# The order of TensorE's products from expert 4 on: down-projections taken one expert later in a mixture-of-experts layer

## The chip, the cores and the metric

The kernel runs on one core of one Trainium2 chip. The metric is the device time of one execution in microseconds (us).

## The reference, cut to what matters

One decoder layer on 256 tokens of width 1024, in float32: a recurrent branch and an attention branch, merged, and then a mixture of 32 experts of which each token takes four. For this case only the experts matter. Per expert, on the tokens routed to it:

```
gu = xb @ w_gu[e] + b_gu[e]                      # w_gu[e]: 1024 x 2048
x_glu = jnp.minimum(gu[:, :D_EXPERT], SWIGLU_LIMIT)
x_lin = jnp.clip(gu[:, D_EXPERT:], -SWIGLU_LIMIT, SWIGLU_LIMIT)
act = x_glu * jax.nn.sigmoid(SWIGLU_ALPHA * x_glu) * (x_lin + 1.0)
return act @ w_down[e] + b_down[e]               # w_down[e]: 1024 x 1024
```

The results are weighted by the router's gates and added up per token.

## The kernel before

The branches come first (products in split float32, weights passing through a landing buffer). From about 280 us on the kernel is a loop over the 32 experts, numbered 0 to 31. Every expert has 64 slots for its tokens; a further pass exists for more and isn't taken here.

**Buffers.** An expert's gate-and-up weights (`gu`, 8 MB) lie in one of two sets, by the parity of the expert, each of two halves of 4 MB. The down weights (`dn`, 4 MB) have one set only, of two halves of 2 MB, which every expert uses.

**The queue of weights.** SP issues all loads, in one order written out by hand (L348 to L352): `gu` of expert 2i, `dn` of 2i-1, `gu` of 2i+1, `dn` of 2i. Ahead of each half it waits until that half's buffer has been read: for `gu` (`load_gu`, L277) on `gu_used`, which TensorE counts up at each quarter of `up`, and for `dn` (`load_dn`, L285) on `dn_used`, counted up at each half of `down`. A wait holds all that stands behind it in SP's program. Experts 0 to 3 have `gu` loads of their own (`load_early`, L269), issued by quarters.

**TensorE** takes per expert e these groups; the lines are those in the profile:

- `up`: the bias (L668), then 32 products with `gu` (L680, 64 records), into banks 4 and 5
- `turn_weights` (L689): two transposes of the weighted selection, which ScalarE copies to `wT`
- `gather` (L620): 48 small products that fetch the tokens of expert e+1, which VectorE copies to `xg`
- `turn_act` (L695): four transposes of the activation, which VectorE made from banks 4 and 5 and then copies to `actT`
- `down`: two halves of 8 products with `dn` (L701, 32 records in all), into bank 6, which ScalarE copies to `y_sb`
- `combine` (L654): the result of the expert before, weighted, into banks 0 to 3

**Two orders.** Up to expert 21 TensorE runs `expert` (L706): `up(e)`, turns and gather, the combine of e-1, and then `down(e)`, for which it waits on weights that lie in the queue behind `gu` of e+1. From expert 22 on it runs `step` (L738): `up(e)`, the gather, then `down(e-1)`, then the turns and the combine of e-1; so `down(e)` stands behind `up(e+1)`, as in the queue. The first step has no `down`. `last_step` ends the loop with expert 31, whose down weights have buffers of their own. ScalarE has the same two bodies (L1003 and L1024), and VectorE the same work in both, with the gather's result in bank 6 or 7. The constant `STEPS` says at which expert the second order begins, on all three engines. SP doesn't use it.

Of the kernel before, what the change touches and what calls it, by code (L numbers as in the profile page):

```python
# [43 lines left out]
ALPHA = 1.702  # L44
CONV = 4
LAND = 2
STEPS = 22
LAST_ROWS = ((0, 2), (2, 3), (3, 4))
N_BLK = 20
PIECES = 4  # L50
# [8 lines left out]
def program(nc, x, vecs, rope, w_in, lru_wx, lru_wa, w_proj_rnn, w_proj_attn, w_out,  # L59
# [7 lines left out]
    with ctx:  # L67
# [176 lines left out]
        def most_rows(eng):  # L244

            eng.wait_ge(count_ready, 1)
            return eng.value_load(cnt_i[0:1, 0:1], min_val=0, max_val=T)
# [175 lines left out]
        def _(pe):  # L423
            mm = nc.tensor.matmul

            def keep_clock(bank, n):

                for _ in range(n):
                    mm(ps[:, bank, :], ones[:, :], ones[:, :].unsqueeze(1).to_broadcast([P, 4, P]),
                       start=True, stop=True)  # L430
# [185 lines left out]
            def gather(buf, bank=6):  # L616

                for k in range(KT):
                    for n, (t, q) in enumerate((t, q) for t in range(TT) for q in range(3)):
                        last = mm(ps[:, bank, k * SLOTS:(k + 1) * SLOTS], part[q][:, t, k * P:(k + 1) * P],  # L620
                                  sel[buf][:, t, :], start=n == 0, stop=n == 3 * TT - 1)
                last.then_inc(gathered, 1)
# [28 lines left out]
            def combine(par, t, y=y_sb, stop=False):  # L651

                for h in range(2):
                    last = mm(ps[:, 2 * t + h, :], wT[par][64 * h:64 * h + 64, t * P:(t + 1) * P],  # L654
                              y[64 * h:64 * h + 64, :], start=False, stop=stop)
                return last

            def up(E, X, par, first=False, early=0):

                if first:  # L660
                    pe.wait_ge(xg_half, 1)
                else:
                    pe.wait_ge(xg_ready, X + (par + 1))
                pe.wait_ge(gu_read, E + (par + 1))
                for c in range(2):
                    for h in range(2):
                        rows = slice(32 * (2 * c + h), 32 * (2 * c + h) + 32)
                        mm(ps[64 * h:64 * h + 64, 4 + c, :], bsel[par][rows, :], b4[rows, :], start=True, stop=False)  # L668
                for m in range(4):
                    if early:  # L670
                        pe.wait_ge(early_landed[par][m], 16 * early)
                    elif m % 2 == 0:
                        pe.wait_ge(gu_landed[par][m // 2], 8 * E - 16)
                    if first and m == 2:
                        pe.wait_ge(xg_ready, 1)
                    for r in range(2):
                        k = 2 * m + r
                        for c in range(2):
                            for h in range(2):
                                last = mm(ps[64 * h:64 * h + 64, 4 + c, :], xg[:, k * SLOTS:(k + 1) * SLOTS],  # L680
                                          gu[par][m // 2][:, m % 2 * 2 + r, c * D + h * HALF:c * D + (h + 1) * HALF],
                                          start=False, stop=k == KT - 1)
                    last.then_inc(gu_used, 1)

            def turn_weights(X, par, bank=7):
                pe.wait_ge(parts_ready, TT)
                pe.wait_ge(sel_ready, X + (par + 1))
                for t in range(TT):
                    last = nc.tensor.transpose(ps[:, bank, t * P:(t + 1) * P], sel_g[par][:, t, :], ident[:, :])  # L689
                last.then_inc(wT_filled, 1)  # L690

            def turn_act(E, par):
                pe.wait_ge(act_ready, E + (par + 1))
                for j in range(4):
                    last = nc.tensor.transpose(ps[:, 7, j * P:(j + 1) * P], act_s[:, j * P:(j + 1) * P], ident[:, :])  # L695
                last.then_inc(actT_filled, 1)

            def down(half, bank=6, src=actT, js=range(DN_RUN), dn=dn):
                for j in js:
                    for h in range(2):  # L700
                        last = mm(ps[64 * h:64 * h + 64, bank, :], src[:, j, half * SLOTS:(half + 1) * SLOTS],  # L701
                                  dn[half][:, j, h * HALF:(h + 1) * HALF],
                                  start=half == 0 and j == 0, stop=half == 1 and j == DN_RUN - 1)
                return last

            def expert(E, X, par, meanwhile=None, first=False, at_once=False, early=0):  # L706

                up(E, X, par, first, early)  # L710
                turn_weights(X, par)
                pe.wait_ge(sel_ready, X + (par + 2))
                if not first:
                    pe.wait_ge(y_ready, E + par)
                gather(1 - par)
                pe.wait_ge(wT_ready, E + (par + 1))
                if meanwhile:
                    meanwhile()
                elif at_once:
                    keep_clock(7, 5)  # L720
                if not (first or at_once):
                    combine(1 - par, 0)
                turn_act(E, par)
                if first or at_once:
                    keep_clock(4, 3)
                else:
                    combine(1 - par, 1)
                pe.wait_ge(actT_ready, E + (par + 1))
                pe.wait_ge(xg_ready, X + (par + 2))
                for half in range(2):  # L730
                    pe.wait_ge(dn_landed[half], 16 * E + 16 * (par + 1) - 16 * at_once)
                    down(half).then_inc(dn_used, 1)
                if at_once:
                    pe.wait_ge(y_ready, E + (par + 1))
                    combine(par, 0)
                    combine(par, 1)

            def step(E, par, first=False):  # L738

                pe.wait_ge(wT_ready, E + par)  # L740
                up(E, E, par)
                pe.wait_ge(actT_ready, E + par)
                pe.wait_ge(sel_ready, E + (par + 2))
                gather(1 - par, 7)
                if not first:
                    for half in range(2):
                        pe.wait_ge(dn_landed[half], 16 * (E + par))
                        down(half).then_inc(dn_used, 1)
                pe.wait_ge(gu_read, E + (par + 2))
                turn_weights(E, par, 5)  # L750
                pe.wait_ge(xg_ready, E + (par + 2))
                turn_act(E, par)
                pe.wait_ge(y_ready, E + par)
                combine(1 - par, 0)
                combine(1 - par, 1)
# [30 lines left out]
            most = most_rows(pe)  # L786
            for par in range(2):
                expert(2, 2, par, early=2)
            with pe.Fori(2, STEPS // 2, 1) as i:
                for par in range(2):  # L790
                    expert(2 * i, 2 * i, par)
            step(STEPS, 0, first=True)
            step(STEPS, 1)
            with pe.Fori(STEPS // 2 + 1, N_E // 2 - 1, 1) as i:
                for par in range(2):
# [23 lines left out]
        def _(act):  # L819
# [199 lines left out]
            most = most_rows(act)  # L1019
            with act.Fori(1, STEPS // 2, 1) as i:  # L1020
                for par in range(2):
                    expert(2 * i, par)

            def step(E, par, first=False):  # L1024
                act.wait_ge(glu_ready, E + (par + 1))
                A(act_s[:, :], g1[:, :], ACT.Sigmoid, scale=ALPHA).then_inc(sig_ready, 1)  # L1026
                if not first:
                    act.wait_ge(dn_used, 2 * E + 2 * par)
                    A(y_sb[:, :], ps[:, 6, :], ACT.Copy).then_inc(y_ready, 1)
                act.wait_ge(wT_filled, E + (par + 1))  # L1030
                A(wT[par][:, :], ps[:, 5, 0:T], ACT.Copy).then_inc(wT_ready, 1)

            step(STEPS, 0, first=True)
            step(STEPS, 1)
# [454 lines left out]
```

## Time and profile before

| | us |
|---|---|
| median of 3 runs | 1199.77 (1198.56 to 1199.92) |
| the profiled execution | 1201.84 |
| its span, first to last instruction | 1200.1 |
| TensorE busy in the span | 1131.4 (94%) |
| VectorE busy | 348.4 (29%) |
| ScalarE busy | 218.6 (18%) |
| mean rate of all DMA | 375 GB/s |

Times in the rows are microseconds from the first instruction. PE is TensorE's products, PEld its weight loads, DVE is VectorE, ACT is ScalarE, SPq is SP's queue. A busy span of TensorE is modelled at its end. The chain of waits is followed back from the last instruction, at each step to what released it. Durations come from this one execution, whose own time is 2.07 us above the median.

### The profile page before, as it was taken

To read this page: it belongs to the slowest core of one execution; us is meant where nothing else is said; L and a number is where in the kernel's file an instruction comes from. 1 tells how busy PE (TensorE), PEld (TensorE's weight loads), DVE (VectorE), ACT (ScalarE), POOL (GpSimd) and SP (SyncE) were. 2 spreads that over 40 slices of the span, in tenths; PEclk is the share of its full clock that TensorE was granted. 3 is DMA by queue.
4 is the path that set the end of the run, shared out by engine and by line. 5 is a ranking of instruction groups with operands and counts; after the bars stand their busy time and mean duration, and the time that the engine had idled before them with its cause. 6 is when DMAs were issued, how large, how long until landed. Compare 5 with 4: busy or idle time off the path is not lost.

```text
span 1200.1 us, 17281 instructions
## 1 busy us (share of the span) xinstructions
PE 1131.4 (94%) x7486; PEld 579.1 (48%) x7486; DVE 348.4 (29%) x667; ACT 218.6 (18%) x359; POOL 5.4 (0%) x20
## 2 busy tenths in 40 slices
PE   8999999999999999999999999999999999999997
PEld 8999899995333333333333333333333333333332
DVE  6747775655221111111111111111111211111112
ACT  5557456444000000000000000000000000000002
POOL 1000000000000000000000000000000000000000
PEclk9999999999999999999999999999999999999999
DMA  9635455798999999999999999999999999999994
GB/s 272 218 142 162 164 219 200 266 361 350 419 413 428 434 429 428 435 428 430 431 429 433 430 427 435 428 428 431 431 430 429 421 428 432 431 429 430 433 428 196
DMA packets 47708, 449.70 MB, mean 375 GB/s; under 512 B 6321, under 2 KB 9457, under 8 KB 30193
## 3 DMA queue, kind: packets, MB, share of 16 engines
q1 hardware_dynamic: 47104, 447.70, 89.5%
q10 hardware_dynamic: 416, 0.83, 0.4%
q8 instruction: 35, 0.57, 0.2%
q0 software_dynamic: 144, 0.52, 0.1%
q14 instruction: 9, 0.07, 0.0%
HBM read 447.48 MB, written 1.05 MB: 374 GB/s over the span
## 4 chain that ended last, share of the span: by engine, by line
PE 49%; DMA 44%; DVE 4%; ACT 2%; issue 1%; SPq 0%; ACTq 0%; DVEq 0%; POOL 0%; POOLq 0%
DMA dn<-in_w_down 34%; PE ps L680 14%; PE ps L701 13%; DMA gu<-in_w_gu 10%; PE ps L456 4%; PE ps L452 4%; PE ps L453 4%; PE ps L654 1%; PE ps L620 1%; DVE w_lo L1106 1%; PE ps L668 1%; PE ps L471 1%; PE ps L472 1%; PE ps L476 1%; PE ps L435 1%
## 5 line engine op out<-in xcount | busy, mean ns | idle before, releaser
L680 PE MATMUL ps<-gu,xg 128*64 128x512 f32 x2048 | 450.9, 597 | 10.2 <-DMA gu<-in_w_gu 10.0
L680 PEld LDWEIGHTS ps<-gu,xg 128*64 128x64 f32 x2048 | 144.5, 138 | 314.5 <-issue 297.3
L701 PE MATMUL ps<-dn,actT 128*64 128x512 f32 x992 | 223.5, 597 | 39.5 <-DMA dn<-in_w_down 39.3
L1398 DVE TENSOR_SCALAR g<-ps 128x512 f32<-128x512 f32 x32 | 22.1, 692 | 674.5 <-PE ps L680 674.5
L701 PEld LDWEIGHTS ps<-dn,actT 128*64 128x64 f32 x992 | 66.9, 137 | 186.7 <-issue 115.9
L1106 DVE TENSOR_TENSOR w_lo<-land,w_hi 128x1024 fp32r<-128x1024 f32 x80 | 94.6, 1219 | 64.1 <-ACT w_hi L842 64.1
L452 PE MATMUL ps<-x_hi,w_hi 128*128 128x256 f32 x384 | 96.3, 288 | 2.4 <-ACTq L880 2.4
L453 PE MATMUL ps<-x_lo,w_hi 128*128 128x256 f32 x384 | 94.8, 284 | 0.0
L842 ACT ACTIVATE w_hi<-land 128x1024 fp32r<-128x1024 f32 x80 | 80.1, 1052 | 51.7 <-PE ps L456 32.7
L452 PEld LDWEIGHTS ps<-x_hi,w_hi 128*128 128x128 f32 x384 | 74.1, 193 | 2.8 <-ACTq L880 2.6
L453 PEld LDWEIGHTS ps<-x_lo,w_hi 128*128 128x128 f32 x384 | 74.1, 193 | 0.1
L654 PE MATMUL ps<-y_sb,wT 64*128 64x512 f32 x248 | 67.6, 633 | 0.7 <-ACT y_sb L1046 0.7
L1005 ACT ACTIVATE wT<-ps 128x256 f32<-128x256 f32 x22 | 8.4, 384 | 317.9 <-PE ps L689 317.9
L1011 ACT ACTIVATE y_sb<-ps 128x512 f32<-128x512 f32 x22 | 13.1, 597 | 271.7 <-PE ps L701 271.7
L456 PE MATMUL ps<-x_hi,w_lo 128*128 128x256 f32 x384 | 54.7, 286 | 0.0
L620 PEld LDWEIGHTS ps<-sel,part 128*128 128x128 bf16 x1488 | 46.9, 98 | 7.6 <-issue 7.3
L456 PEld LDWEIGHTS ps<-x_hi,w_lo 128*128 128x128 f32 x384 | 50.3, 195 | 0.0
L620 PE MATMUL ps<-sel,part 128*128 128x64 bf16 x1488 | 48.5, 193 | 0.0
L1409 DVE COPY actT<-ps 128x512 f32<-128x512 f32 x31 | 21.4, 691 | 55.9 <-PE ps L695 53.5
L1026 ACT ACTIVATE act_s<-g 128x512 f32<-128x512 f32 x9 | 5.7, 630 | 166.9 <-DVE g L1398 166.9
L668 PE MATMUL ps<-b,bsel 32*64 32x512 f32 x256 | 34.8, 613 | 0.0
L654 PEld LDWEIGHTS ps<-y_sb,wT 64*128 64x128 f32 x248 | 19.4, 185 | 13.5 <-issue 9.5
(258 smaller groups left out, 836.8 us busy)
## 6 DMA issues: line engine op xcount, KB each, us to landing
gu<-in_w_gu SPq DMA_DIRECT2D x56, 4096.0 KB, 28.5
dn<-in_w_down SPq DMA_DIRECT2D x62, 2048.0 KB, 25.3
gu<-in_w_gu SPq DMA_DIRECT2D x16, 2048.0 KB, 13.5
land<-in_w_in SPq DMA_DIRECT2D x13, 2048.0 KB, 8.4
land<-in_w_proj_rnn SPq DMA_DIRECT2D x2, 2048.0 KB, 9.1
land<-in_w_proj_attn SPq DMA_DIRECT2D x2, 2048.0 KB, 9.9
land<-in_w_out SPq DMA_DIRECT2D x2, 2048.0 KB, 7.8
dn_last<-in_w_down SPq DMA_DIRECT2D x1, 2048.0 KB, 26.7
```

The costliest lines, as they stand in the source:

```text
L452: mm(to, w_hi[:, b, k, :], src_hi[:, k, :], start=k == 0, stop=False)
L453: mm(to, w_hi[:, b, k, :], src_lo[:, k, :], start=False, stop=False)
L456: last = mm(to, w_lo[:, b, k, :], src_hi[:, k, :], start=False, stop=k == KT - 1)
L620: last = mm(ps[:, bank, k * SLOTS:(k + 1) * SLOTS], part[q][:, t, k * P:(k + 1) * P], sel[buf][:, t, :], start=n == 0, stop=n == 3 * TT - 1)
L654: last = mm(ps[:, 2 * t + h, :], wT[par][64 * h:64 * h + 64, t * P:(t + 1) * P], y[64 * h:64 * h + 64, :], start=False, stop=stop)
L668: mm(ps[64 * h:64 * h + 64, 4 + c, :], bsel[par][rows, :], b4[rows, :], start=True, stop=False)
L680: last = mm(ps[64 * h:64 * h + 64, 4 + c, :], xg[:, k * SLOTS:(k + 1) * SLOTS], gu[par][m // 2][:, m % 2 * 2 + r, c * D + h * HALF:c * D + ...
L701: last = mm(ps[64 * h:64 * h + 64, bank, :], src[:, j, half * SLOTS:(half + 1) * SLOTS], dn[half][:, j, h * HALF:(h + 1) * HALF], start=ha ...
L842: A(w_hi[:, q % PIECES], land[u % LAND][:, :, (q % PIECES) * P:(q % PIECES + 1) * P], ACT.Copy).then_inc(hi_ready, 1)
L1106: V.tensor_tensor(w_lo[:, p], land[q // PIECES % LAND][:, :, p * P:(p + 1) * P], w_hi[:, p].bitcast(f32), ALU.subtract).then_inc(lo_ready, 1)
L1398: V.tensor_scalar(by_rows(g1[:, :]), by_columns(ps[:, 4, :]), LIMIT, None, ALU.min).then_inc(glu_ready, 1)
L1409: V.tensor_copy(to[:, :, :], ps[:, 7, :].rearrange("p (j s) -> p j s", j=4)).then_inc(actT_ready, 1)
```

## The change

The constant goes from 22 to 4, and TensorE's loop over the pairs of experts 4 to 21 in the first order goes, as it would be empty. Experts 2 and 3 stay in the first order. On ScalarE and VectorE the loop bounds follow from the constant: their first loop then holds experts 2 and 3 alone, and the second one the pairs from 4 or 6 on.

```diff
@@ -44,7 +44,7 @@
 CONV = 4
 LAND = 2
-STEPS = 22
+STEPS = 4
 LAST_ROWS = ((0, 2), (2, 3), (3, 4))
@@ -786,9 +786,6 @@
             for par in range(2):
                 expert(2, 2, par, early=2)
-            with pe.Fori(2, STEPS // 2, 1) as i:
-                for par in range(2):
-                    expert(2 * i, 2 * i, par)
             step(STEPS, 0, first=True)
             step(STEPS, 1)
             with pe.Fori(STEPS // 2 + 1, N_E // 2 - 1, 1) as i:
```

## Rows read from the trace of the kernel before

**Rows 1.** The page: what the DMA engines moved, in 40 equal slices of 30 us.
```profile
GB/s 272 218 142 162 164 219 200 266 361 350 419 413 428 434 429 428 435 428 430 431 429 433 430 427 435 428 428 431 431 430 429 421 428 432 431 429 430 433 428 196
```

**Rows 2.** The chain that ended last: start, length, what (L701 `down`, L680 `up`).
```profile
500.90 3.68 PE ps L701 x16
...
884.74 25.34 DMA dn<-in_w_down
910.12 3.65 PE ps L701 x16
...
1047.96 7.09 PE ps L680 x32
...
1125.03 39.78 DMA gu<-in_w_gu
1164.85 8.63 PE ps L680 x32
```

**Rows 3.** Timeline of TensorE, experts 4 and 5: start, length, instructions.
```profile
394.03 13.95 PE L680 MATMUL ps<-gu,xg 128*64 128x512 f32 x64
...
412.47 7.09 PE L701 MATMUL ps<-dn,actT 128*64 128x512 f32 x32
...
420.51 13.95 PE L680 MATMUL ps<-gu,xg 128*64 128x512 f32 x64
```

**Rows 4.** Timeline of TensorE, experts 22 to 24, in the second order.
```profile
914.72 13.95 PE L680 MATMUL ps<-gu,xg 128*64 128x512 f32 x64
...
935.64 13.95 PE L680 MATMUL ps<-gu,xg 128*64 128x512 f32 x64
...
951.03 7.09 PE L701 MATMUL ps<-dn,actT 128*64 128x512 f32 x32
...
961.79 13.96 PE L680 MATMUL ps<-gu,xg 128*64 128x512 f32 x64
```

**Rows 5.** Timeline of SP's queue, `dn` of experts 23 and 24.
```profile
954.90 3.75 SPq L285 DMA_DIRECT2D dn<-in_w_down  x2
...
981.01 3.77 SPq L285 DMA_DIRECT2D dn<-in_w_down  x2
```

**Rows 6.** Timeline of SP's queue, `dn` of expert 5.
```profile
416.34 3.75 SPq L285 DMA_DIRECT2D dn<-in_w_down  x2
```

**Rows 7.** Tile `gu`, 408 to 409 us: expert 6's second half, issue to landing.
```profile
L277 SPq DMA_DIRECT2D gu<-in_w_gu x1: 333/333/333, 408.2 to 408.2; - x1
...
DMA to landing us min/median/max: 24.5/24.5/24.5
```

**Rows 8.** Tile `dn`, 247.5 to 248.5 us: a half of expert 0.
```profile
L285 SPq DMA_DIRECT2D dn<-in_w_down x1: 347/347/347, 247.9 to 247.9; - x1
...
DMA to landing us min/median/max: 7.6/7.6/7.6
```

**Rows 9.** Tile `dn`, 416 to 417 us: expert 5's first half.
```profile
L285 SPq DMA_DIRECT2D dn<-in_w_down x1: 333/333/333, 416.3 to 416.3; - x1
...
DMA to landing us min/median/max: 21.2/21.2/21.2
```

**Rows 10.** Tile `dn`, 340 to 341 us, and below it `gu`, 348 to 349.
```profile
L285 SPq DMA_DIRECT2D dn<-in_w_down x1: 328/328/328, 340.2 to 340.2; - x1
...
DMA to landing us min/median/max: 12.0/12.0/12.0
...
L277 SPq DMA_DIRECT2D gu<-in_w_gu x1: 353/353/353, 348.4 to 348.4; - x1
...
DMA to landing us min/median/max: 16.1/16.1/16.1
```

**Rows 11.** Timeline of TensorE, second halves of `up` of experts 28 and 29.
```profile
1077.18 7.09 PE L680 MATMUL ps<-gu,xg 128*64 128x512 f32 x32 [2.63 <-DMA gu<-in_w_gu]
...
1106.42 8.78 PE L680 MATMUL ps<-gu,xg 128*64 128x512 f32 x32 [2.63 <-DMA gu<-in_w_gu]
```

**Rows 12.** Window 1106.4 to 1108: busy times, PEclk granted, DMA share, GB/s.
```profile
1106.40:1108.00 1.60, 1.58 (x4) 0.44 (x6) 0.00 (x0) 0.00 (x0) 0.00 (x0) 0.55 1.11 471
```

## The prediction

> **What bounds the kernel now.** I read three views in turn. The page's slices say what is full: from the eleventh slice on, 300 us, each slice but the last moves 413 to 435 GB/s [rows 1], the flat ceiling of the expert loop. So the first question for any change here is whether it lets this stream pause. The chain of waits says who ends last in each stretch. Over experts 7 to 21 it repeats one pair: a `dn` transfer, then the second half of `down` that waited for it [rows 2]. Those waits end at 500.90 for expert 7 and at 910.12 for expert 21: 409.22 us for 14 experts, 29.23 us each. That is the pace of the weights: three equal parts of 4 MB a turn, so 9.74 us for 4 MB and 4.87 us for 2 MB. Near the end the chain goes through `gu` transfers to 1164.85, where TensorE starts the second half of expert 31's gate-and-up product; what follows is a fixed tail [rows 2].
>
> The timeline of TensorE says what an expert costs it when nothing is late. In the old order `up` of expert 4 starts at 394.03 and that of expert 5 at 420.51: 26.48 us [rows 3]. In the new order, experts 23 to 24, it is 961.79 - 935.64 = 26.15 us [rows 4]. Both are under 29.23, so from expert 7 on TensorE waits for weights in either order, and its order can't shorten the stream. It can only lengthen it, by freeing a buffer too late, or change the tail.
>
> **The change part by part.** Experts 4 to 21 leave the old body for the new one. The products per expert are the same (64 records of `up`, 32 of `down`, 48 of the gather and so on), no DMA is added or dropped, and the last experts already run in the new order. The moved step is `down(e)`: from before `up(e+1)` to behind it. What it releases, `dn_used`, is what SP waits for ahead of the next `dn` issue, and behind that wait in SP's program stand the next two `gu` halves. So a late `down` holds back 12 MB of transfers, even where the `gu` buffers have long been free.
>
> *The steady part* costs nothing. In the new order before, SP issues the `dn` halves of successive turns at 954.90 and 981.01, 26.11 us apart, faster than the weights' 29.23 [rows 5], so SP gains about 3.1 us of lead per turn until TensorE is held by weights again. The 0.33 us a turn that TensorE saves lies under that wait.
>
> *The first turns* are the matter, because at expert 4 TensorE is still behind the weights. Where is the new release? `up(4)` keeps its start of 394.03. The short first step takes 935.64 - 914.72 = 20.92 us [rows 4], so `up(5)` starts at 414.95 in place of 420.51. `down(4)` comes 951.03 - 935.64 = 15.39 us later, at 430.34 in place of 412.47 [rows 3, 4]. SP issues `dn(5)` 954.90 - 951.03 = 3.87 us after `down` starts [rows 4, 5], at 434.21 in place of 416.34 [rows 6]. When is the queue empty? The last transfer ahead, the second half of `gu(6)`, is issued at 408.2 and lands 24.5 us later, at 432.7 [rows 7]; it is released by `up(4)`, which doesn't move. So the queue runs dry 1.5 us before the next issue. Then `dn(5)` restarts it cold. A 2 MB `dn` half issued at 247.9, just as the queue had emptied, took 7.6 us to land [rows 8], against 4.87 behind other transfers; so it lands at 441.8. In the old order it landed at 416.3 + 21.2 = 437.5 [rows 9]. **First term: +4.3 us.**
>
> The Trainium skill (DMA: Bandwidth & Descriptors, section "Anatomy of one DMA") gives a transfer a fixed part of about 2.0 us beside its bytes, most of it the receipt after the last byte. By that page 2 MB would land after 6.8 us (an estimate), the term would be 3.5 us, and since a receipt doesn't delay the transfer behind it, the stream itself would lose less still. The row's 7.6 us is this kernel's own and I keep it.
>
> *The thin queue after a restart.* A queue that is short, though not empty, also lost time. At the switch by expert 22 the weights' own schedule puts the end of `gu(24)` at 910.12 plus four halves of `gu` (experts 23 and 24) and two of `dn(22)`, that is 910.12 + 4 x 9.74 + 2 x 4.87 = 958.8; `dn(23)` was issued at 954.90, a lead of 3.9 us. The stream lost something even so: from 910.12 to the landing of `gu(27)`'s second half, which TensorE waited for until 1047.96, lie ten `gu` halves and eight `dn` halves, 97.4 + 39.0 = 136.4 us, and it took 137.84. **That is 1.4 us lost at today's switch** [rows 2, 5], and the second issue's lead of 7 to 8 us (981.01 against 988.0) is within it. A worse case is expert 4's `gu`: issued at 348.4, when the `dn` ahead of it landed at 340.2 + 12.0 = 352.2, it landed at 364.5 [rows 10]: 12.3 us for a transfer of 9.74, so 2.6 us lost with 3.8 us of lead.
>
> After the restart, `dn(5)`'s second half and the two halves of `gu(7)` are issued within some 5 us with leads of 4 us and up, as at 954.90. Between 0 (the thin part is already in the cold restart) and 2.6 I take 1.4, the case with the same code. **Second term: +1.4 us.** The next turn: `up(6)` starts at 414.95 + 26.15 = 441.10, so `dn(6)` is issued at 441.10 + 15.39 + 3.87 = 460.4. The queue, shifted by 5.7 us, holds work to 461.9 + 5.7 = 467.6 (461.9 is 442.4 for `dn(5)`'s second half plus two `gu` halves). The lead is 7.2 us, like the second issue at today's switch, whose cost is in the 1.4; at most another 1.4. The turn after that has 10 us, and it grows.
>
> **Third term: -1.4 us**, today's loss at expert 22, which goes away, since there TensorE already waits for weights in the new order and SP's issues are far ahead of the stream.
>
> Sum: 4.3 + 1.4 - 1.4 = **+4.3 us**. Nothing later takes it back: from 442 to 1164 the stream is full, and the tail hangs on its last pieces. Against the profiled execution's own 1201.84 us (span 1200.1) that gives 1206.1; that execution is 2.1 us above the median of the runs shown. On the median, 1199.77 + 4.3 = **1204.1**.
>
> *The tail and the clock.* With one long wait per turn in place of two short ones, TensorE stood idle 2.63 us in mid-`up`. After one such gap, at 1077.18, the half took 7.09 us; after another, at 1106.42, it took 8.78 [rows 11]; in the slow stretch the granted clock was 0.55, close to the lower of its two levels, 1.2 against 2.4 GHz [rows 12]. Expert 31's half took 8.63 [rows 2]. In mid-loop the 1.7 us hide under the 3.1 us of slack; in the last half they are on the path. I expect it in the new kernel as well, and so no difference; but if it falls away there it gives back 1.5 us. [...]
>
> **The rivals.** *The queue doesn't miss it.* TensorE's late release is covered, or the switch costs the same 1.4 us wherever it stands: then 1199.8, or 1198.3 without the last dip. For it: today's switch costs 1.4. Against it: there the lead was 3.9 us, here it is -1.5, and 1.5 comes from rows in direct sequence; this case holds from the point where `dn(5)` is issued before 432.7 - 3.9 = 428.8. *Faster*: the new order at 22 had cost its 1.4 and this goes, the pause at expert 5 is absorbed, and the last half runs at the full clock: 1.4 + 1.5 = 2.9, so 1196.9. It needs a queue that is fed past 434 by what is now behind the wait; rows 7 speak against it. *A deeper pause*: each of the next two issues loses like the worst row, 4.3 + 2.6 + 1.4 - 1.4 = 6.9, so 1206.7; for it: three issues in a row with leads under 8 us; against it: only the first was seen to lose much. *The clock falls at every expert*, and in both halves of `up`: 1.6 us each, 26.15 + 3.2 = 29.35 a turn, just over the weights' 29.23, so about 0.1 us a turn for 25 turns, +3 us on top: 1207. [...]
>
> **How the numbers follow.** Forecast 62%; not missed 24%; faster 5%; deeper pause 7%; clock 2%. The forecast's own bounds are 4.3 + 0 - 1.4 = 2.9, less 1.5 for the tail, so 1.4 (1201.2), and 6.9 (1206.7). To leave no more than 2 in 10 out, the range goes down past the second case's 1199.8, to 1199.0, and up to 1207.0, which takes the deeper pause in. No change can be told from 0.2%, that is 2.4 us, so slower begins at 1202.2. The forecast with the tail's 1.5 off is 1202.6, still above; its low corner isn't. Slower 0.68, same 0.27, faster 0.05.
>
> **What would show it.** In the changed kernel: `up(5)` at 415, `down(4)` at 430.3, SP's `dn` issue at 434.2 where 416.34 stood; a hole of about 2 us or more in the DMA share after 432; the landing of that half at 441.8 or later; from about expert 8 on, a second half of `up` that waits for `gu`, every 29.2 us, and the last of these, expert 31's, about 4 us behind 1164.85. If no hole is there, or the wait for `gu(31)` ends within 1 us of 1164.85, the forecast is wrong; if the hole is there and the end isn't later, then something in the stream was not at its ceiling.

## The result and the profile after

The changed kernel took 1205.15 us, the median of 6 runs (1201.81 to 1207.55), beside 1199.76 for the kernel before on the same chip: ratio 1.0048, interval 1.0032 to 1.0064. On another chip, in the run e8 below, it was 1.0037 (1.0021 to 1.0052). So the change makes the kernel slower, by 5.4 us on the first chip and 4.1 on the second, by the medians; the forecast was +4.3.

The profiled execution of the changed kernel was its fastest, 1201.81 us with a span of 1200.0, no longer than the span before. Its trace must therefore be read by differences. First the page's 30 us slices:

```profile
GB/s 271 221 141 179 186 215 203 242 389 349 423 410 433 430 338 434 432 426 434 434 426 434 433 427 433 431 428 434 427 430 428 432 430 430 430 430 431 431 429 226
```

One slice stands out against [rows 1]: the fifteenth, 420 to 450 us, with 338 GB/s where 429 stood. The timeline of TensorE there:

```profile
391.00 13.95 PE L680 MATMUL ps<-gu,xg 128*64 128x512 f32 x64
...
411.92 13.95 PE L680 MATMUL ps<-gu,xg 128*64 128x512 f32 x64
...
427.31 3.23 PE L701 MATMUL ps<-dn,actT 128*64 128x512 f32 x14
```

In this execution `up(4)`, the first of these rows, starts 3.03 us earlier than in [rows 3]. From there on the steps are those of [rows 4] to 0.01 us: 20.92 to `up(5)`, 15.39 to `down(4)`. SP's queue:

```profile
398.28 7.19 SPq L277 DMA_DIRECT2D gu<-in_w_gu  x2
431.18 3.75 SPq L285 DMA_DIRECT2D dn<-in_w_down  x2
435.18 0.85 SPq L277 DMA_DIRECT2D gu<-in_w_gu  x2
```

No `dn` issue stands between the `gu` of expert 6 and 431.18; before there was one at 416.34 [rows 6]. The tiles by single windows, the last `gu` ahead and the first `dn` behind:

```profile
L277 SPq DMA_DIRECT2D gu<-in_w_gu x1: 333/333/333, 405.1 to 405.1; - x1
...
DMA to landing us min/median/max: 24.6/24.6/24.6
```

```profile
L285 SPq DMA_DIRECT2D dn<-in_w_down x1: 333/333/333, 431.2 to 431.2; - x1
...
DMA to landing us min/median/max: 7.8/7.8/7.8
```

The queue's last transfer lands at 405.1 + 24.6 = 429.7, and the next is issued 1.5 us later, at 431.2. It lands at 439.0 (438.9 by the unrounded times). The windows of 1 us show the hole itself; the last three columns are the granted clock, the DMA share and GB/s. A packet is counted in the window in which it starts:

```profile
427.00:428.00 1.00, 1.00 (x17) 0.60 (x15) 0.93 (x3) 0.28 (x1) 0.00 (x0) 1.00 0.15 49
428.00:429.00 1.00, 1.00 (x6) 0.29 (x4) 1.00 (x2) 0.00 (x0) 0.00 (x0) 1.00 0.00 0
429.00:430.00 1.00, 1.00 (x8) 0.35 (x6) 0.26 (x1) 0.00 (x0) 0.00 (x0) 1.00 0.00 0
430.00:431.00 1.00, 1.00 (x8) 0.37 (x6) 0.00 (x0) 0.00 (x0) 0.00 (x0) 1.00 0.00 0
431.00:432.00 1.00, 1.00 (x6) 0.29 (x4) 0.00 (x0) 0.00 (x0) 0.00 (x0) 1.00 0.00 0
432.00:433.00 1.00, 1.00 (x8) 0.35 (x6) 0.00 (x0) 0.00 (x0) 0.00 (x0) 1.00 1.22 229
```

In four windows no packet starts, while TensorE is busy in all of them. By the packets' own times in the trace nothing is in flight from 429.2 to 432.15, 2.9 us. By TensorE's own row nothing is wrong here.

What the stream lost: with 3.03 us taken off, the old order's landing of `dn(5)` would be 437.5 - 3.0 = 434.5, so it is 4.4 us late. `gu(7)` then landed at 454.4, 15.5 us after that `dn` half, where 4.87 + 9.74 = 14.6 are its due, and `dn(6)`'s second half came another 0.5 late. In all the stream is 5.8 us behind by 480, and then keeps its pace to the end:

```profile
1126.01 39.97 DMA gu<-in_w_gu
1166.02 7.09 PE ps L680 x32
```

The last wait for `gu` ends at 1166.02, 1.17 us after 1164.85 [rows 2]: 5.8 lost at expert 5, 1.4 not lost at expert 22, 3.0 gained ahead of the loop, which makes +1.4; 0.2 is what my readings leave. The profile of e8, which starts its loop when the kernel before does, has this wait end at 1168.70, 3.85 us behind 1164.85, where the prediction put it "about 4 us" behind:

```profile
1168.70 8.78 PE ps L680 x32
```
The 3.0 us ahead of the loop in the first profile aren't the change's: no code there differs. They go with the clock. These windows are of the changed kernel, and then of the kernel before:

```profile
10.00:20.00 10.00, 7.96 (x66) 7.72 (x65) 9.55 (x23) 8.54 (x16) 0.00 (x0) 1.00 1.12 334
...
120.00:140.00 20.00, 17.04 (x139) 16.73 (x138) 17.68 (x22) 8.71 (x12) 0.00 (x0) 1.00 0.50 180
```

```profile
10.00:20.00 10.00, 7.59 (x51) 7.35 (x50) 9.59 (x25) 7.21 (x13) 0.00 (x0) 0.83 1.13 333
120.00:140.00 20.00, 17.05 (x126) 16.48 (x126) 17.67 (x22) 9.92 (x12) 0.00 (x0) 0.91 0.58 205
```

A granted clock of 0.83 over 10 us and of 0.91 over 20 us is about 1.7 us of full clock withheld each time, 3.4 in all before, and nothing after. The twelve traces of this case agree: in the first 280 us six have nothing withheld, and `up(0)` starts at 281.1 to 281.7; three have 1.7 us, and it starts at 282.4 to 283.2; two have 3.4, 284.1 and 284.3; one has 5.1, 285.4. And expert 31's half took 7.09 us after against 8.63 before: another 1.5. So this one execution had luck worth about 4.5 us, which hides the change in its span. The median of the runs doesn't have it.

### The profile page after: what moved, and what is told of

Same layout as the page of the kernel before. It is cut to its first block, busy times and chain, and to the rows that moved or that the text cites. A ratio compares the mean times of both kernels' runs of the same rounds, so it can differ in the third digit from the quotient of the medians.

```text
span 1200.0 us, 17253 instructions
## 1 busy us (share of the span) xinstructions
PE 1132.4 (94%) x7486; PEld 578.5 (48%) x7486; DVE 348.5 (29%) x667; ACT 217.0 (18%) x359; POOL 5.4 (0%) x20
## 4 chain that ended last, share of the span: by engine, by line
PE 54%; DMA 38%; DVE 4%; ACT 2%; SPq 1%; issue 1%; ACTq 0%; DVEq 0%
DMA gu<-in_w_gu 37%; PE ps L680 19%; PE ps L701 12%; PE ps L452 4%; PE ps L456 4%; PE ps L453 4%; PE ps L620 2%; PE ps L654 1%; DVE w_lo L1103 1%; PE ps L668 1%; PE ps L476 1%; PE ps L471 1%; PE ps L472 1%; ACT w_hi L839 1%; SPq L277 0%
## 5 line engine op out<-in xcount | busy, mean ns | idle before, releaser
L680 PE MATMUL ps<-gu,xg 128*64 128x512 f32 x2048 | 465.9, 610 | 47.2 <-DMA gu<-in_w_gu 46.7
L680 PEld LDWEIGHTS ps<-gu,xg 128*64 128x64 f32 x2048 | 145.6, 140 | 366.1 <-issue 287.8
L701 PE MATMUL ps<-dn,actT 128*64 128x512 f32 x992 | 219.9, 595 | 0.1
L701 PEld LDWEIGHTS ps<-dn,actT 128*64 128x64 f32 x992 | 68.5, 137 | 128.3 <-issue 124.1
L1023 ACT ACTIVATE act_s<-g 128x512 f32<-128x512 f32 x27 | 17.0, 630 | 535.7 <-DVE g L1395 535.7
L654 PE MATMUL ps<-y_sb,wT 64*128 64x512 f32 x248 | 62.7, 618 | 0.7 <-ACT y_sb L1043 0.7
L1026 ACT ACTIVATE y_sb<-ps 128x512 f32<-128x512 f32 x26 | 15.5, 598 | 186.3 <-PE ps L701 186.3
L1398 DVE SCALAR_TENSOR_TENSOR l<-l,g 128x512 f32<-128x512 f32 x32 | 22.1, 692 | 1.1
```

The lines of the kernel that those rows point to most:

```text
L1398: V.scalar_tensor_tensor(out=l1[:, :], in0=l1[:, :], scalar=1.0, in1=g1[:, :], op0=ALU.add, op1=ALU.mult).then_inc(t_ready, 1)
```

## The experiments

Each ratio is to the kernel before on the same chip. The first four ran together, then the next four, then the last two.

**Switch two experts later (e1_steps6).**

```diff
-STEPS = 22
+STEPS = 6
```

> STEPS = 6 in the kernel before: the new order two experts later. Dry-queue theory: the lead of the first late dn issue grows by 29.23 - 26.48 = 2.75 us per expert, so from -1.5 us (switch at 4) to about +4, the same as at 22 (3.9): no hole, and the time of the kernel before within 0.2%, 1199 to 1201.5 us. Rival, the new order itself costs in each of its experts (clock falls, waits inside up): 26 of the 28 experts of the changed kernel still run in it, so about +5 us, 1204 to 1205.

Measured: 1200.09 us, ratio 1.0008 (0.9996 to 1.0020). Moving the switch by two experts takes most or all of the loss away, though 26 of 28 experts run in the new order. The expected lead of 4 us wasn't there in the profile: `dn` was issued at 486.0, with the queue's last landing at 487.4, a lead of 1.4, and that half came 2.3 us late.

```profile
L285 SPq DMA_DIRECT2D dn<-in_w_down x1: 333/333/333, 486.0 to 486.0; - x1
...
DMA to landing us min/median/max: 8.6/8.6/8.6
```

Some 1.6 us of the missing 2.6 are in the first step. It took 466.72 - 444.16 = 22.56 us in place of 20.92, and a window in it shows the clock lowered:

```profile
460.00:470.00 10.00, 8.44 (x36) 2.91 (x38) 3.09 (x9) 0.36 (x1) 0.00 (x0) 0.83 1.03 439
```

Another 0.8 is that the stream had lost less before expert 4: 1.9 us late there in this trace, 2.6 in the kernel before. With 2.3 late at the switch and 0.3 behind it, against 1.5 behind the switch of the kernel before, this trace would make e1 1.1 us slower, and the interval holds that.

**Issue the next `gu` ahead of the late `dn` (e2_gu_ahead).** The changed kernel, and SP's turn of experts 6 and 7 written out apart:

```diff
                 load_gu(i * (2 * D), 0, ...)
-                load_dn(i * (2 * D) - D, ...)          # dn(5), waits for down(4)
                 load_gu(i * (2 * D) + D, 1, ...)       # gu(7)
+                load_dn(i * (2 * D) - D, ...)
                 load_dn(i * (2 * D), ...)
```

> The changed kernel with SP's order changed at one place: both gu halves of expert 7 are issued ahead of dn of expert 5, which waits for the late down. TensorE's order stays. Dry-queue theory: gu(7) is issued 10 and 4 us before the queue would run dry, so no hole, and most of the 5.8 us that the hole and what follows it cost come back: 1198 to 1201 us. Rival, the order of TensorE costs the time: 1204 to 1206, as the changed kernel. Rival, dn(5) now lands later than TensorE wants it (by some 5 us) and that wait is passed on: 1203 or more.

Measured: 1200.38 us, ratio 1.0017 (1.0004 to 1.0030). TensorE's order is that of the changed kernel, and by the medians more than half of the loss is gone (its interval overlaps that of e8 below, not that of the first result). Nine of the twelve runs took 1198.9 to 1202.1 us; the other three took 1204.4 to 1205.1 and have the lowest granted clocks, 0.979 to 0.981. The trace has no hole: `dn(5)` is issued at 431.1 as in the changed kernel, but with 16.7 us of work ahead of it in the queue. So the loss is in the queue, not in the order of the products. What remains is the second rival in part: `dn(5)` now lands later than `down(5)` wants it.

```profile
453.97 3.65 PE L710 MATMUL ps<-dn,actT 128*64 128x512 f32 x16 [0.31 <-DMA dn<-in_w_down]
458.83 3.65 PE L710 MATMUL ps<-dn,actT 128*64 128x512 f32 x16 [1.20 <-DMA dn<-in_w_down]
```

That holds `down(5)` up, and with it the issue of `dn(6)`, whose leads are then 1.1 and 2.7 us; its halves land 1.5 and 0.8 us late.

**Hold the late `down` for 3 us more (e3_after_held), and the same in the kernel before (e4_before_held).**

```diff
+                if held:                  # held=14, at expert 4's down alone
+                    keep_clock(6, held)   # products of ones into bank 6
                 for half in range(2):
                     pe.wait_ge(dn_landed[half], ...)
```

> The changed kernel, with 14 products of ones (about 3 us) ahead of the first moved down, that of expert 4; they go to a bank that is overwritten. Dry-queue theory: the issue of dn(5) is 3 us later, the hole 3 us longer, and the end 3 us later: 1207 to 1209 us. Rival, TensorE's lateness is absorbed by the slack of 3 us per expert that follows: no change, 1204 to 1206.

> The kernel before, with the same 14 products (about 3 us) ahead of the same down, that of expert 4. Its dn(5) issue has 16 us of lead, which falls to 13: no loss, within 0.2% of the kernel before, 1199 to 1201. If TensorE's time is on the path at this place in either order: about 3 us slower, 1203.

Measured: in the changed kernel 1208.19 us, ratio 1.0074 (1.0060 to 1.0089); in the kernel before 1200.80, ratio 1.0006 (0.9993 to 1.0018). The products took 3.19 us in the first trace. `dn(5)` was issued at 436.1 against a last landing at 430.3, 5.7 us dry in place of 1.5, and landed 8.4 us late in place of 4.4. Of the 4.2 us more, the products account for 3.0 (`down(4)` starts 18.42 us after `up(5)` in place of 15.39); in addition the landing ahead came 1.2 us sooner after `up(4)` than in the first profile.

```profile
L285 SPq DMA_DIRECT2D dn<-in_w_down x1: 332/332/332, 436.1 to 436.1; - x1
...
DMA to landing us min/median/max: 7.5/7.5/7.5
```

In the kernel before the same 3 us left a lead of 11.9 us, and `dn(5)` landed exactly in turn (417.9 + 16.8 = 434.7, 4.9 after `gu(6)` at 429.8). The same lateness of TensorE, at the same product, is worth 3 to 4 us in one order and nothing measurable in the other. That is the rival "the slack that follows absorbs it" ruled out for the new order.

**The changed kernel again (e8_after_again)**, with no edit.

> The changed kernel once more, to have it beside the others on one chip. Dry-queue theory: 4 to 6 us above the kernel before (the hole of the first profile cost the stream 5.8 us against today's switch at 22 with about 1.4), and the hole after the landing of gu(6) in its profile again. If the first result was a matter of that chip or of those few runs of before: within 2 us of the kernel before.

Measured: 1203.48 us, 12 runs, ratio 1.0037 (1.0021 to 1.0052). Its profile has the hole at its place:

```profile
L285 SPq DMA_DIRECT2D dn<-in_w_down x1: 333/333/333, 434.0 to 434.0; - x1
...
DMA to landing us min/median/max: 7.9/7.9/7.9
```

Last landing ahead 432.6, issue at 434.0, landing 4.4 us late at 441.9, and `gu(7)` another 0.9 late. Here `up(0)` started at 284.13, as before (284.33), and the end, a span of 1204.3, is 4.2 us later than the span before.

**Switch at expert 12 (e7_steps12).**

```diff
-STEPS = 22
+STEPS = 12
```

> STEPS = 12 in the kernel before. TensorE has been waiting for weights for five experts by then, as at 22, so the lead of the first late dn issue is 3.9 us as at 22, and the time that of the kernel before within 0.1%. A thin queue as such costs 1.4 us here too, right behind the switch; if the 1.4 us seen at 22 was something else, the landings follow each other in 9.7 and 4.9 us. If the new order costs in each of its experts: 20 of 28, so +3 to +4 us.

Measured: 1198.26 us, ratio 0.9991 (0.9976 to 1.0005): no difference, as in e1. By the interval, 20 experts in the new order cost 0.6 us at most. The lead at the switch was 3.8 us, and a landing behind it came late again, by 1.0 us: the second half of a `gu` that had been issued 18.8 us ahead of its turn. The short lead's own `dn` had landed in time.

**A fuller queue at the old switch (e6_half_ahead_fill), and the clock in the tail (e5_fill).** e5 is the kernel before with products in the wait in mid-`up` of experts 28 to 31; e6 has in addition half of expert 25's `gu` ahead of `dn` of expert 23:

```diff
                 for m in range(4):
+                    if m == 2 and fill:       # fill=10
+                        keep_clock(6, fill)
```

```diff
                 load_gu(i * (2 * D), 0, ...)
+                if ahead:                     # i == 12 alone
+                    load_gu(i * (2 * D) + D, 1, second, [0])
                 load_dn(i * (2 * D) - D, ...)
-                load_gu(i * (2 * D) + D, 1, second)
+                load_gu(i * (2 * D) + D, 1, second, [1] if ahead else range(2))
```

> The kernel before, with 10 products of ones (2.3 us, into a bank that is overwritten) in the middle of up in experts 28 to 31, where TensorE waits 2.6 us for the second gu half. Clock theory: the granted clock stays at its upper level after that wait, expert 31's half takes 7.1 us in place of 8.6 in all runs, and the median falls by the share of runs that had the fall, 0.5 to 1.5 us. Rival: the clock is not bound to these waits, or the products themselves run into the wait: no change or up to 1 us slower.

> The same, and SP issues the first gu half of expert 25 ahead of dn of expert 23, behind the switch at 22. The lead of dn(23) is then 13 us in place of 3.9. If a thin queue costs 1.4 us at the switch: another 1 to 1.4 us faster than with the products alone. If those 1.4 us have another cause: the same time as with the products alone.

Measured: e5 1198.82 us, ratio 0.9990 (0.9976 to 1.0004); e6 1199.22, ratio 0.9996 (0.9982 to 1.0009). In e5's profile the wait before expert 31's half is filled, and the half runs in 7.09 us:

```profile
1158.46 2.33 PE L430 MATMUL ps<-ones 128*128 128x512 bf16 x10
1161.16 7.09 PE L683 MATMUL ps<-gu,xg 128*64 128x512 f32 x32 [0.37 <-DMA gu<-in_w_gu]
```

The mean granted clock of its 12 runs was 0.994 to 0.999, against 0.990 to 0.996 in the runs of the kernel before on that chip. The gain that this should give, 0.5 to 1.5 us, is inside the interval and not shown. e6 decides the other question. Its `dn(23)` had a lead of 13.7 us in place of 3.8, and the second half of `gu(25)` was still 1.5 us late, issued 19.7 us ahead of its turn:

```profile
L278 SPq DMA_DIRECT2D gu<-in_w_gu x1: 1265/1265/1265, 956.8 to 956.8; - x1
...
DMA to landing us min/median/max: 31.0/31.0/31.0
```

So the 1.4 us at the switch is no matter of a thin queue.

**Fresh code without a switch (e9_fresh_code).** Behind each switch TensorE runs instructions for the first time; the windows of the DMA view show 16 KB transfers of instructions on queue q8 there, and none between 440 and 910 us in the kernel before. This one writes a turn of the old order out between two loops:

```diff
-            with pe.Fori(2, STEPS // 2, 1) as i:
+            with pe.Fori(2, 8, 1) as i:
                 for par in range(2):
                     expert(2 * i, 2 * i, par)
+            for par in range(2):
+                expert(16, 16, par)
+            with pe.Fori(9, STEPS // 2, 1) as i:
+                for par in range(2):
+                    expert(2 * i, 2 * i, par)
```

> The kernel before, with TensorE's code for experts 16 and 17 written out between two loops in place of being one more turn of the loop. Order, waits and products are the same. If the 1 to 1.6 us lost behind each switch come from loading code that TensorE has not run yet (16 KB transfers on queue q8 beside the weights): such transfers appear at about 740 to 830 us, where the kernel before has none, a landing there comes 1 to 2 us late, and the time is 1 to 2 us above the kernel before. If they come from the switch itself (the order, the leads): landings stay 4.9 and 9.7 us apart there, and the time is the same.

Measured: 1200.40 us, ratio 1.0006 (0.9992 to 1.0020). The time can't tell 1 us. The trace can. Between 740 and 840 us five windows of 10 us have an instruction transfer; this is the one at 780:

```profile
q1 hardware_dynamic: 268, 4.13, 97.1%
q8 instruction: 1, 0.02, 0.7%
```

And one landing in that stretch is late, by 1.3 us, of a `gu` half issued at 783.5 with 20.1 us of lead; the one issued at 754.3, and all others from 700 to 900, keep their distances to 0.1 us:

```profile
L277 SPq DMA_DIRECT2D gu<-in_w_gu x1: 332/332/332, 754.3 to 754.3; - x1
...
DMA to landing us min/median/max: 29.9/29.9/29.9
```

```profile
L277 SPq DMA_DIRECT2D gu<-in_w_gu x1: 333/333/333, 783.5 to 783.5; - x1
...
DMA to landing us min/median/max: 31.2/31.2/31.2
```

A second trace agrees, though it was made for something else. To hold one `down`, e4 has the turn of experts 4 and 5 written out ahead of the loop. It has instruction transfers between 450 and 500 us, where the kernel before has none, and there one `dn` half lands 1.5 us late, with a lead of 18.9 us:

```profile
L285 SPq DMA_DIRECT2D dn<-in_w_down x1: 333/333/333, 474.3 to 474.3; - x1
...
DMA to landing us min/median/max: 25.3/25.3/25.3
```

**Both small gains together (e10_steps12_fill).** STEPS = 12 and the products of e5.

> STEPS = 12 with the 10 products of ones in the middle of up of experts 28 to 31: the two versions that came out 0.9991 and 0.9990 of the kernel before, together. If both small gains are real they add: 0.998, 1 to 2.5 us faster than the kernel before. If they are chance: within 1 us of it.

Measured: 1199.25 us, ratio 1.0001 (0.9988 to 1.0014). They don't add; 0.9991 and 0.9990 were chance, or gains too small for these runs to show. No version here is shown to beat the kernel before.

## Why the prediction was right

**What bounds it.** Right. The weights' stream sets the time from 300 us on, and neither order shortens it: e1, e7 and the kernel before agree within their intervals with the new order in 26, 20 and 10 of the last 28 experts.

**The place and the moment.** Right to 0.1 us, once the 3.03 us of the earlier start are taken off: `down(4)` 427.31 + 3.03 = 430.34, issue 431.18 + 3.03 = 434.21, 1.5 us after the last landing. For TensorE's part that is no luck. For the queue's it partly is: over the twelve traces the second half of `gu(6)` lands 37.2 to 39.0 us after `up(4)` starts (38.6 before, 38.7 in both profiles of the changed kernel), so the queue could as well have been dry for 1.2 or for 3.0 us.

**First term, +4.3.** Measured 4.4 to 4.5 in both profiles, 7.8 and 7.9 us from a cold issue to landing against the 7.6 it was worked out from. The experiment e3 shows that it grows with TensorE's lateness, e4 that it doesn't in the old order, and e2 that it goes in good part when the queue is fed by something else. The Trainium skill (DMA: Bandwidth & Descriptors, "Anatomy of one DMA") gives its fixed part of about 2.0 us for transfers that GpSimd issues, and these are issued by SP. By its figures 2 MB would land after 6.8 us (an estimate) and the term would be 3.5, both too low here. Nor does this trace show most of the fixed part behind the last byte: the last packet ends at 429.2 and its transfer lands at 429.7, 0.5 us later, while 1.0 us passes from the issue at 431.18 to the first packet at 432.15. That 1.0 us is the same in e8, in e3 and at 247.9 in the kernel before.

**Second and third term, +1.4 and -1.4.** The sizes were near: 1.4 (0.9 and 0.5) in the first profile, 0.9 in e8. The step that failed is the one that called them "the thin queue after a restart". A short lead costs something by itself, but only below the leads at hand: leads of 1.1, 1.4, 2.5 and 2.7 us (e2, e1, e9, e2) gave landings 1.5, 2.3, 0.2 and 0.8 us late, while the 14 `dn` halves issued with 3.8 to 5.5 us came at most 0.1 late. The losses behind the switches are of another kind. Late landings of 1.0 to 1.5 us came with leads of 18.8 (before and e7), 19.7 (e6) and 20.1 us (e9). What they have in common is an instruction transfer. Between 340 and 1145 us the twelve traces have 35 landings more than 0.25 us late that aren't behind a hole or a lead under 3 us, and in each of the 35 an instruction transfer is in flight between the landing before and this one. The prediction's worst row, 2.6 us at 364.5 [rows 10], is one of them. The reverse doesn't hold: there are 173 such transfers in that stretch of the traces, and most have no late landing beside them. That they belong to code that TensorE meets first is shown by e9 and e4; how one transfer of 16 KB could hold a landing up for over 1 us stays open.

The two terms cancelled, then, for another reason than was given, the late landing going where the switch goes, and that they cancelled so well is luck: behind the same switch at 22 these late landings sum to 1.5 us in the kernel before, 1.8 in e9 and nothing in e4.

**The tail and the clock.** The fall comes and goes: 8.63 us before, 7.09 in the first profile after, 8.78 in e8, 7.09 in e4, with the same wait of 2.6 us before it or, in e4, 1.64. To expect no difference was right. In e1 the first step, which waits 1.6 us for its tokens, was 1.6 us longer with the clock lowered; such a fall ahead of the first late `dn` would lengthen the hole, but no trace here has one there. The changed kernel's runs reach from 1201.2 to 1207.6, and over its 18 runs the time goes with the mean granted clock: 0.986 in the three at or below 1201.81, 0.980 in the three above 1207. The kernel before spreads as much, 1195.6 to 1203.4 us with granted clocks from 0.996 to 0.990, so this is not the new order's doing; the falls ahead of the loop, told above, are a part of it.

**The rivals.** "The queue doesn't miss it" fell by the hole itself. "Faster" had its parts seen (a tail at full clock, a start 3 us earlier), but by luck of one execution and with the hole in it. "A deeper pause" didn't come: at the second issue the lead was 6.8 us, its first half lost nothing and its second 0.5. "The clock falls at every expert" is ruled out: in the changed kernel's two profiles the clock fell in 9 and 10 of the 28 experts from 4 on, always in the second half of `up`, and the next expert's wait for `gu` was then 1.2 to 1.5 us in place of 2.6. So the weights' pace hid it, and e1 and e7, with 26 and 20 experts in that order, lose nothing by it.

## What to carry to other kernels

When one queue feeds a kernel, work out for each wait in the issuing program how long the queue still has to run when that wait ends; that lead, not the consumer's slack, prices a reordering. Here the same reordering costs 4 to 5 us where the lead is -1.5 us and nothing that can be measured where it is 4. A wait in the issuing program holds back all transfers behind it, also those whose buffers are free; to issue one of these first is a cheap way to test the cause. And a single profiled execution can carry several microseconds of luck, so compare it by the distances between events and not by its span.

## What the runs showed that I had not expected

A stream that keeps 9.74 and 4.87 us between landings to 0.1 us over hundreds of microseconds has single landings 1.0 to 1.5 us late however long the queue is, and in twelve traces every one of these had an instruction transfer beside it. And the same instructions ahead of the expert loop took 281.3 us in one execution and 284.3 in another, with 3.4 us less of granted clock in the slower.
